# Four unread matmuls on the tensor engine ahead of the first product behind each of six norms

## The chip, the cores and the metric

The kernel runs as one program on one core of a Trainium2 chip. The metric is the device time of one execution in microseconds (us), as the median of several runs. The engines of the core are named as the profile names them: PE is the tensor engine's matmuls and PEld its weight loads, DVE the vector engine, ACT the scalar engine, POOL the GpSimd engine, SP the engine whose queue carries the weight transfers. PE works at one of two granted clock levels, 2.4 GHz (written as 1.00 in the profile) and 1.2 GHz (0.50).

## What the reference computes

The input x has 512 tokens of 1024 features in float32. It goes through six blocks one after the other, each as a residual:

```python
h = h + nsa_mixer(rmsnorm(h, l0_norm))          # attention, three branches
h = h + s5_mixer(rmsnorm(h, l1_norm))           # state-space scan
h = rmsnorm(h, final_norm)
h = h + even_mixer(rms_norm(h, mix_norm_g[0]))  # stick-breaking and retention
h = h + conv_ffn(rms_norm(h, ffn_norm_g[0]))
h = h + odd_mixer(rms_norm(h, mix_norm_g[1]))   # gated linear attention
h = h + conv_ffn(rms_norm(h, ffn_norm_g[1]))
```

A norm is `x * rsqrt(mean(x*x) + 1e-6) * gain` over the features of a token. Seven norms stand in the program; six of them are followed at once by a large product with a weight matrix (`w_in` of the four mixers, `w_up` of the two feed-forward layers), and one, the final norm of the first half, is followed by another norm.

## The kernel before, in words

**Layout.** All activations are kept feature-major: `h` is 128 partitions by 8 chunks by 512 tokens. Sums over features are matmuls with a 128x128 matrix of ones (`ones`, a part of the tile `tables`), which leave the sum on every partition.

**Products.** The weights come as tiles of 128 outputs (128 x 1024 numbers, 512 KB). SP loads them into a ring of four buffers `raw` (line 131). DVE rounds a tile to `whi` (line 155) and POOL forms the rest `wlo = raw - whi` (line 149); both are double buffered. The activations are split in the same way into `xh` and `xl`. One output tile is then 8 chunks of three matmuls, `whi*xh`, `whi*xl`, `wlo*xh`, 24 in all, into one of two accumulators `acc[0]`, `acc[1]`, which are banks 0 and 1. A tile's end is counted on `tile_done`, on which DVE waits to round the tile after next, and ACT or DVE to take the accumulator; whoever takes it counts on `acc_free`.

**Norms.** ACT squares the chunks of `h` (line 202), DVE adds them up in `ssq` (line 215). At a stage's end `pe_squares` (lines 217 to 224) multiplies `ones` by `ssq` and by the last square, two matmuls in plain float32. In the profile one plain float32 matmul shows as two records. `act_rstd` takes the logarithm and the exponential (lines 232, 234). Then `dve_norm` (line 251 makes `xf`, line 255 makes `xl`) and `act_norm_split` (line 241 makes `xh`) go through the 8 chunks in four rounds of two, with two buffers `xf`.

**The first products.** `products_from_norm` (line 258) issues the first four tiles of the stage behind a norm. In its first tile every chunk waits for that chunk's `xl` (the semaphore `norm_lo`); lines 269, 270 and 271 are its three matmuls. It is called for six stages: `nsa_kv`, `s5_in`, `even_in`, `up0`, `odd_in`, `up1`. What PE has in its program just ahead of the call differs:

- `nsa_kv`: 32 plain float32 matmuls for the gates (line 1033), each chunk's behind its `xf`; they all stand ahead of the call.
- `even_in`: a wait for three transfers of tables, `pe.wait_ge(e_loaded, 48)` (line 554). ACT issues them behind its share of the norm (lines 651 to 653).
- `odd_in`: the gate matmul (line 1563) of each chunk is inside the call, ahead of that chunk's three matmuls of the first tile. DVE waits for it (semaphore `o_gmm`) before it writes that `xf` buffer again.
- `s5_in`, `up0`, `up1`: nothing but `pe_squares`.

PE's program is one stream in order, so whatever stands in it is done before what follows it.

Of the kernel before, what the change touches and what calls it, by code (L numbers as in the profile page):

```python
# [36 lines left out]
def plan(names):  # L37

    t0, o0, n, t, o = {}, {}, {}, 0, 0
    for name, tiles, per_output in STAGES:  # L40
        if name not in names:
            continue
        t0[name], o0[name], n[name] = t, o, tiles
        t, o = t + tiles, o + tiles // per_output
    return t0, o0, n, t


def build(nc, A, out, names=tuple(s[0] for s in STAGES)):
    T0, O0, NT, TILES = plan(names)
# [4 lines left out]
    with ExitStack() as ctx:  # L54
        def sb(name, shape, dt=F32):
            return ctx.enter_context(nc.sbuf_tensor(name, shape, dt))

        def sem(name):
            return ctx.enter_context(nc.semaphore(name))
# [3 lines left out]
        acc = bank[0:2]  # L63
        ssum = bank[7]

        h = sb("h", [P, KC, S])
# [13 lines left out]
        ones = tables[:, 0:P]  # L80
# [18 lines left out]
        acc_free = [sem("acc_free0"), sem("acc_free1")]  # L99
# [143 lines left out]
        def dve_norm(dve, n, view=lambda x: x, reader=None):  # L243

            dve.wait_ge(rstd_ready, n + 1)
            with dve.Fori(0, KC // 2) as i:
# [6 lines left out]
                for j in range(2):  # L253
                    dve.wait_ge(norm_hi, i * 2 + (8 * SPLIT[n] + j + 1))
                    nc.vector.tensor_tensor(chunk(xl, i * 2 + j), xf[:, j, :], chunk(xh, i * 2 + j).bitcast(F32),
                                            ALU.subtract).then_inc(norm_lo, 1)

        def products_from_norm(pe, stage, n, beside=None, between=None):

            for j in range(4):  # L260
                pe.wait_ge(w_lo, T0[stage] + j + 1)
                pe.wait_ge(acc_free[j % 2], (O0[stage] + j) // 2 + 1)
                for k in range(KC):
                    if j == 0:
                        if beside is not None:
                            beside(k)
                        pe.wait_ge(norm_lo, 8 * SPLIT[n] + k + 3)
                    w_h, w_l = whi[:, j % 2, k * P:(k + 1) * P], wlo[:, j % 2, k * P:(k + 1) * P]
                    nc.tensor.matmul(acc[j % 2][:], w_h, xh[:, k, :], start=k == 0, stop=False)  # L269
                    nc.tensor.matmul(acc[j % 2][:], w_h, xl[:, k, :], start=False, stop=False)  # L270
                    mm = nc.tensor.matmul(acc[j % 2][:], w_l, xh[:, k, :], start=False, stop=k == KC - 1)  # L271
                mm.then_inc(tile_done, 1)
                if between is not None:
                    between(j)
# [65 lines left out]
        def pe_ffn(pe, layer):  # L340
            products_from_norm(pe, f"up{layer}", ORDER[(N_FFN0, N_FFN1)[layer]])
            products_feature_major(pe, f"up{layer}", 4, 2 * FT - 4)
            third = FT - 2 * KC
            rhs = [(lambda k, q=q: ghi[:, q * KC + k, :], lambda k, q=q: glo[:, q * KC + k, :]) for q in range(3)]
            after = ORDER[(N_FFN0, N_FFN1)[layer]] + 1
            pe_residual(pe, f"down{layer}", after if after < len(norms) else None,
                        lambda k: pe.wait_ge(g_lo, FT * layer + k + 1), 3, rhs, (KC, KC, third))
# [205 lines left out]
        def pe_even(pe):  # L553
            pe.wait_ge(e_loaded, 48)
            products_from_norm(pe, "even_in", ORDER[N_MIX0], between=lambda j: pe_head_squares(pe, 0) if j == 2 else None)
            parts = iter(range(16, 28 * 4))

            def beside(n):
                for _ in range(n):
                    product_beside(pe, "even_in", 0, 0, 4, next(parts))  # L560

            for i in range(4):
                pe_stick(pe, i, beside)
                pe_retention(pe, i, beside if i < 3 else lambda n: pe_even_out_beside(pe, n))
# [461 lines left out]
        def pe_nsa(pe):  # L1026
# [11 lines left out]
            for m in range(KC):  # L1038
                gate(m)
            products_from_norm(pe, "nsa_kv", n)  # L1040
            products_feature_major(pe, "nsa_kv", 4, 4)

# [1648 lines left out]
```

## Time and profile before

| | |
|---|---|
| median of 3 runs | 2185.01 us (2181.14 to 2190.68) |
| the profiled execution's own time | 2186.51 us |
| its span, first to last instruction | 2184.7 us |
| mean granted PE clock | 0.964 |
| PE busy | 92% of the span |
| DVE, ACT, POOL busy | 53%, 32%, 37% |

The span is 1.8 us shorter than the execution's own time, and that execution is 1.5 us above the median. Times in a timeline are counted from the span's start. A row of a timeline gives start, duration, engine, line, operation and tiles, and in brackets how long the engine sat idle before it and what ended that. The duration of a matmul record holds the time its last column takes to come out; the distance of two starts is what a matmul costs in a row of them.

### The profile page before, as it was taken

To read this page: it belongs to the slowest core of one execution; us is meant where nothing else is said; L and a number is where in the kernel's file an instruction comes from. 1 tells how busy PE (TensorE), PEld (TensorE's weight loads), DVE (VectorE), ACT (ScalarE), POOL (GpSimd) and SP (SyncE) were. 2 spreads that over 40 slices of the span, in tenths; PEclk is the share of its full clock that TensorE was granted. 3 is DMA by queue.
4 is the path that set the end of the run, shared out by engine and by line. 5 is a ranking of instruction groups with operands and counts; after the bars stand their busy time and mean duration, and the time that the engine had idled before them with its cause. 6 is when DMAs were issued, how large, how long until landed. Compare 5 with 4: busy or idle time off the path is not lost.

```text
span 2184.7 us, 28177 instructions
## 1 busy us (share of the span) xinstructions
PE 2004.5 (92%) x9960; PEld 1574.4 (72%) x9960; DVE 1155.3 (53%) x2011; ACT 697.6 (32%) x1284; POOL 799.1 (37%) x412
## 2 busy tenths in 40 slices
PE   5999999777999985999988999999998898999999
PEld 4777777656777764666666888888586676888887
DVE  5728998676994443555535555522513435555411
ACT  2125655223552122444413333300313423333200
POOL 1451221234773431222223444444242133444443
PEclk8999999898999997999989999999999999999999
DMA  3630110211211221111112222233221022222232
GB/s 116 171 109 30 40 40 20 77 61 54 68 33 68 96 87 63 58 58 59 58 49 79 96 96 96 96 106 106 69 87 58 29 70 77 96 96 96 96 125 77
DMA packets 55150, 167.56 MB, mean 77 GB/s; under 512 B 8065, under 2 KB 16129, under 8 KB 54801
## 3 DMA queue, kind: packets, MB, share of 16 engines
q1 hardware_dynamic: 47760, 155.22, 21.2%
q10 hardware_dynamic: 7296, 11.08, 1.8%
q8 instruction: 62, 1.02, 0.2%
q14 instruction: 32, 0.25, 0.0%
HBM read 157.88 MB, written 2.10 MB: 73 GB/s over the span
## 4 chain that ended last, share of the span: by engine, by line
PE 56%; issue 24%; DVE 11%; POOL 6%; ACT 1%; ACTq 1%; DMA 0%; DVEq 0%; POOLq 0%
PE bank L164 13%; PE bank L166 13%; PE bank L165 13%; POOL wlo L149 6%; DVE prob L1416 2%; DVE ssb L1403 2%; PE bank L269 1%; PE bank L270 1%; PE bank L271 1%; DVE sb__137 L2078 1%; PE bank L1135 1%; DVE sb__137 L2073 1%; PE bank L492 1%; PE bank L1160 1%; PE bank L493 1%
## 5 line engine op out<-in xcount | busy, mean ns | idle before, releaser
L149 POOL TENSOR_TENSOR wlo<-raw,whi 128x1024 fp32r<-128x1024 f32 x260 | 626.6, 2410 | 1134.4 <-DVE whi L155 1134.4
L155 DVE CAST whi<-raw 128x1024 fp32r<-128x1024 f32 x288 | 202.7, 704 | 641.4 <-PE bank L166 449.4
L164 PE MATMUL bank<-xh,whi 128*128 128x512 f32 x832 | 328.1, 394 | 12.9 <-POOL wlo L149 9.7
L165 PE MATMUL bank<-xl,whi 128*128 128x512 f32 x832 | 326.5, 392 | 0.0
L166 PE MATMUL bank<-xh,wlo 128*128 128x512 f32 x832 | 326.2, 392 | 0.0
L164 PEld LDWEIGHTS bank<-xh,whi 128*128 128x128 f32 x832 | 157.9, 190 | 48.3 <-POOL wlo L149 11.4
L166 PEld LDWEIGHTS bank<-xh,wlo 128*128 128x128 f32 x832 | 157.9, 190 | 33.4
L165 PEld LDWEIGHTS bank<-xl,whi 128*128 128x128 f32 x832 | 158.1, 190 | 32.7
L492 PE MATMUL bank<-xh,whi 128*128 128x512 f32 x328 | 140.5, 428 | 2.2 <-ACT oin L478 1.2
L164 PE MATMUL bank<-ghi,whi 128*128 128x512 f32 x352 | 136.9, 389 | 0.0
L166 PE MATMUL bank<-ghi,wlo 128*128 128x512 f32 x352 | 136.9, 389 | 0.0
L165 PE MATMUL bank<-glo,whi 128*128 128x512 f32 x352 | 136.9, 389 | 0.0
L494 PE MATMUL bank<-xh,wlo 128*128 128x512 f32 x328 | 129.4, 394 | 0.0
L493 PE MATMUL bank<-xl,whi 128*128 128x512 f32 x328 | 129.2, 394 | 0.0
L269 PE MATMUL bank<-xh,whi 128*128 128x512 f32 x192 | 83.2, 433 | 38.2 <-DMA swap<-in_swap_dram 19.5
L381 DVE SCALAR_TENSOR_TENSOR c<-upad,cw,c 128x512 f32<-128x512 f32 x44 | 77.0, 1750 | 56.0 <-ACT c L361 56.0
L1464 POOL TENSOR_TENSOR wlo<-raw,whi 128x1024 fp32r<-128x1024 f32 x20 | 47.2, 2361 | 149.2 <-DVE whi L155 149.2
L202 ACT ACTIVATE bank<-h 128x512 f32<-128x512 f32 x42 | 25.2, 601 | 220.2 <-DVE h L306 212.5
L1416 DVE TENSOR_SCALAR prob<-prob,gsig,stat 128x128 f32<-128x128 f32 (+3 forms) x128 | 87.2, 723 | 2.3
L391 DVE TENSOR_TENSOR glo<-gf,ghi 128x512 f32 x44 | 66.1, 1501 | 40.9 <-ACT ghi L366 40.9
L269 PEld LDWEIGHTS bank<-xh,whi 128*128 128x128 f32 x192 | 38.7, 201 | 64.8 <-DMA swap<-in_swap_dram 21.1
L492 PEld LDWEIGHTS bank<-xh,whi 128*128 128x128 f32 x328 | 62.4, 190 | 24.9 <-issue 11.6
(362 smaller groups left out, 3962.5 us busy)
## 6 DMA issues: line engine op xcount, KB each, us to landing
raw<-in_weights_dram SPq DMA_DIRECT2D x288, 512.0 KB, 3.6
h<-in_x_dram SPq DMA_DIRECT2D x1, 2048.0 KB, 8.3
sz<-su SPq DMA_DIRECT2D x128, 16.0 KB, 1.8
out_dram<-h ACTq DMA_DIRECT2D x4, 512.0 KB, 3.2
etab<-in_even_tables_dram ACTq DMA_DIRECT2D x1, 1730.0 KB, 6.4
x_kh<-kvc_h ACTq DMA_DIRECT2D x2, 256.0 KB, 4.0
x_kl<-kvc_l ACTq DMA_DIRECT2D x2, 256.0 KB, 5.5
x_vh<-kvc_h ACTq DMA_DIRECT2D x2, 256.0 KB, 8.3
```

The source lines that it names most:

```text
L149: nc.gpsimd.tensor_tensor(wlo[:, s % 2, :], raw[:, s, :], whi[:, s % 2, :].bitcast(F32), ALU.subtract).then_inc(w_lo, 1)
L155: nc.vector.tensor_copy(whi[:, t_of_4 % 2, :], raw[:, t_of_4, :]).then_inc(w_hi, 1)
L164: nc.tensor.matmul(to, w_h, pe_h, start=first and k == 0, stop=False)
L165: nc.tensor.matmul(to, w_h, pe_l, start=False, stop=False)
L166: last_mm = nc.tensor.matmul(to, w_l, pe_h, start=False, stop=last and k == chunks - 1)
L269: nc.tensor.matmul(acc[j % 2][:], w_h, xh[:, k, :], start=k == 0, stop=False)
L381: nc.vector.scalar_tensor_tensor(c1[:], upad[:, 1:1 + S], cw[:, layer, 1, ds(i * 2 + j, 1)], c0[:], ALU.mult, ALU.add).then_inc(conv1, 1)
L391: nc.vector.tensor_tensor(chunk(glo, i * 2 + j), gf[:], chunk(ghi, i * 2 + j).bitcast(F32), ALU.subtract).then_inc(g_lo, 1)
L492: nc.tensor.matmul(to[:], w_h, xh[:, k, :], start=k == 0, stop=False)
L493: nc.tensor.matmul(to[:], w_h, xl[:, k, :], start=False, stop=False)
L494: mm = nc.tensor.matmul(to[:], w_l, xh[:, k, :], start=False, stop=k == KC - 1)
L1416: mul = nc.vector.tensor_scalar(prob[:, br, hd, 0:w], prob[:, br, hd, 0:w], gsig[:, qb, g:g + 1], stat[:, 8 + 2 * br + hd:9 + 2 * br + hd] ...
```

## The change

A function `pe_keep_busy` is called first in `products_from_norm`, so at all six stages. It waits until the accumulator `acc[0]` is free, which the first product would wait for too, and issues four plain float32 matmuls of `ones` by the first chunk of `h` into it, each of 128x128 by 128x512 and each beginning a new sum. Nobody reads them; the first product begins with `start=True` and overwrites them. Nothing else changes.

```diff
+        KEEP = 4
+
+        def pe_keep_busy(pe, stage):
+
+            pe.wait_ge(acc_free[0], O0[stage] // 2 + 1)
+            for _ in range(KEEP):
+                nc.tensor.matmul(acc[0][:], ones, h[:, 0, :], start=True, stop=True)
+
         def products_from_norm(pe, stage, n, beside=None, between=None):
 
+            pe_keep_busy(pe, stage)
             for j in range(4):
                 pe.wait_ge(w_lo, T0[stage] + j + 1)
                 pe.wait_ge(acc_free[j % 2], (O0[stage] + j) // 2 + 1)
```

## Rows read from the trace of the kernel before

**Rows 1.** The page: busy shares, and the granted clock in 40 slices.

```profile
PE 2004.5 (92%) x9960; PEld 1574.4 (72%) x9960; DVE 1155.3 (53%) x2011; ACT 697.6 (32%) x1284; POOL 799.1 (37%) x412
...
PEclk8999999898999997999989999999999999999999
```

**Rows 2.** The waits of PE: us in total, times, longest.

```profile
PE bank L222 <- DVE ssq L215: 44.7, 7, 23.7
PE bank L269 <- DMA swap<-in_swap_dram: 19.5, 1, 19.5
```

**Rows 3.** Timeline behind the last norm, stage `up1`.

```profile
1811.57 1.02 PE L224 MATMUL bank<-sq,tables 128*128 128x512 f32 x2
...
1816.84 0.76 PE L269 MATMUL bank<-xh,whi 128*128 128x512 f32 x1 [4.25 <-DVE xl L255]
...
1822.60 0.52 PE L269 MATMUL bank<-xh,whi 128*128 128x512 f32 x1
...
1824.77 1.37 DVE L255 TENSOR_TENSOR xl<-xf,xh 128x512 f32 x2 [0.23 <-ACT xh L241]
...
1825.52 0.50 PE L269 MATMUL bank<-xh,whi 128*128 128x512 f32 x1 [1.26 <-DVE xl L255]
```

**Rows 4.** Timeline: plain float32 matmuls of 512 columns.

```profile
823.94 1.91 PE L224 MATMUL bank<-sq,tables 128*128 128x512 f32 x2
...
1555.45 3.69 PE L1572 MATMUL bank<-gas,walpha 16*128 16x512 f32 x8
```

**Rows 5.** Timeline: the first products of `nsa_kv` and `even_in`.

```profile
44.49 0.77 PE L269 MATMUL bank<-xh,whi 128*128 128x512 f32 x1
...
845.38 0.80 PE L269 MATMUL bank<-xh,whi 128*128 128x512 f32 x1 [19.53 <-DMA swap<-in_swap_dram]
...
851.01 0.40 PE L269 MATMUL bank<-xh,whi 128*128 128x512 f32 x1
851.24 0.39 PE L270 MATMUL bank<-xl,whi 128*128 128x512 f32 x1
```

**Rows 6.** Timeline behind the norm of `s5_in`.

```profile
457.12 1.67 PE L224 MATMUL bank<-sq,tables 128*128 128x512 f32 x2
...
463.05 0.77 PE L269 MATMUL bank<-xh,whi 128*128 128x512 f32 x1 [4.27 <-DVE xl L255]
```

**Rows 7.** Timeline behind the norm of `odd_in`.

```profile
1534.66 1.02 PE L224 MATMUL bank<-sq,tables 128*128 128x512 f32 x2
...
1539.06 1.59 PE L1563 MATMUL bank<-xf,wga 128*16 128x512 f32 x2 [3.38 <-DVE xf L251]
...
1542.15 1.33 PE L1563 MATMUL bank<-xf,wga 128*16 128x512 f32 x2
...
1543.67 0.75 DVE L251 SCALAR_TENSOR_TENSOR xf<-h,gains,rstd 128x512 f32<-128x512 f32 x1 [1.80 <-PE bank L1563]
```

**Rows 8.** Stretches between two times: busy us by engine, granted clock.

```profile
core 0: us, PE busy (x) PEld busy (x) DVE busy (x) ACT busy (x) POOL busy (x), PEclk, DMA share, GB/s
...
44.40:47.70 3.30, 3.30 (x10) 2.62 (x10) 2.71 (x13) 0.52 (x4) 0.00 (x0) 0.50 0.00 0
...
463.00:467.50 4.50, 4.22 (x9) 2.96 (x10) 4.01 (x7) 1.31 (x3) 0.00 (x0) 0.50 0.01 2
...
822.50:825.90 3.40, 3.35 (x4) 0.74 (x3) 0.00 (x0) 0.83 (x2) 0.00 (x0) 0.50 0.00 0
825.90:829.30 3.40, 0.00 (x0) 0.00 (x0) 1.46 (x3) 2.07 (x4) 0.00 (x0) 0.99 0.00 0
...
845.30:849.80 4.50, 4.42 (x10) 3.51 (x11) 0.00 (x0) 0.00 (x0) 0.00 (x0) 0.50 0.00 0
...
1167.60:1170.60 3.00, 2.91 (x7) 1.90 (x7) 2.77 (x5) 1.26 (x2) 0.00 (x0) 0.50 0.00 0
...
1815.80:1822.60 6.80, 5.76 (x13) 3.64 (x13) 6.14 (x10) 3.21 (x6) 0.00 (x0) 0.50 0.00 0
1822.60:1828.00 5.40, 4.13 (x17) 3.01 (x18) 3.62 (x7) 1.96 (x3) 0.00 (x0) 0.99 0.06 17
```

## The prediction, made before the changed kernel was run

> **What bounds the kernel now.** I read the page first: PE is busy for 92% of the span and its granted clock is below 9 tenths in only a few slices [rows 1]. So the tensor engine sets the time nearly everywhere, and each us put into its stream where it doesn't wait is a us of the kernel. Next I read whom PE waits for. The pauses ahead of the sum of squares are not touched, since the new matmuls come behind it; the one long wait the change stands near is 19.5 us for the transfer of `swap` ahead of `even_in` [rows 2]. Then I read the timeline behind each of the six norms and asked two questions: is PE idle at the place where the new matmuls stand in its program, and is it PE that sets the pace behind them.
>
> Behind the last norm (`up1`) the second record of the sum of squares starts 0.43 us behind the first, at 1812.0, and makes room for the next at 1812.4. The first product starts at 1816.84. That is the pause the change means, 4.4 us. What follows is not paced by PE: the chunks of the first tile come in pairs, at 1822.60 and again at 1825.52, one pair in 2.92 us, because DVE and ACT make them so; PE waits 1.26 us for the last pair [rows 3]. A pair is six matmuls. They take 6 x 0.23 = 1.4 us at the full clock (two starts 0.23 us apart, [rows 5]), and 6 x 0.44 = 2.6 us at the half clock (10 in 4.42 us, [rows 8]). Both are less than 2.92. So the half clock that the trace shows there, from 1815.8 to 1822.6 [rows 8], delays nothing: the first tile ends when DVE's last `xl`, of the row at 1824.77, is there [rows 3].
>
> **The change, part by part.** It removes nothing. It adds four plain float32 matmuls at six places, a read of `h` that nobody writes there, and a wait for `acc[0]` that the first product has as well and that is fulfilled long before, so I cost it at nothing.
>
> The price of four such matmuls: eight records of exactly this kind, 512 columns one behind the other, took 3.69 us, of which some 0.2 us is the last one coming out, at the full clock; so 8 x 0.43 = 3.4 us [rows 4]. That row has 16 partitions in place of 128; the pair of records of the sum of squares, 1.02 us for two at the full clock [rows 3], gives the same 0.43. At the half clock two records took 1.91 us [rows 4], so a record is 0.85 and the four matmuls 6.8 us.
>
> Now by place.
>
> `nsa_kv`. The 32 gate matmuls stand ahead of the call, and PE goes from them into the first product at 44.49 with no idle time [rows 5]. There is no pause left: every record of the new matmuls lies on the path. The clock is at half until 47.7 [rows 8]. If it rises at the same time as before, the work added is 8 records in an unchanged stretch of slow clock: 3.2 us at half take 3.8 records, the other 4.2 take 1.8 us at full, and the products that had run at half now run at full. Net, the delay is the price at full clock, **+3.4 us**. Bounds: 0 if something behind it has that much slack, 6.8 if the clock rises only later. I take 3.4, as PE's stream behind it is dense and DVE's side work there hangs on each tile's end.
>
> `even_in`. The wait for the tables stands ahead of the call, so the pause of 19.5 us isn't filled at all: the new matmuls start where the first product did, at 845.4, on a cold engine [rows 2, 5]. The clock was at half until 849.8 and then full [rows 8]. By the same working: **+3.4 us**, bounds 0 and 6.8.
>
> `s5_in`. The sum of squares ran partly at half clock, and the next record can start at about 458.6 (the row at 457.12 lasts 1.67 us, less the 0.2 that the last takes to come out). The first product waits for `xl` until 463.05, so there are 4.4 us [rows 6]. At full clock the four fit; at half they would end at 465.4, 2.4 us late. A dense pass of such records did lift the clock before: it was at 0.50 over the sum of squares from 822.5 to 825.9 and at 0.99 right behind it, with no other matmul near [rows 8]. So I expect a rise within the pass, near 460.7, and an end at 463.1. And were it late, the first tile catches up: a pair costs PE 1.4 to 2.6 us and comes every 3. **+0.1 us**, bounds 0 and 0.5.
>
> `up0` and `up1`. 3.4 us in a pause of 4.4 at the full clock: they end a us before the first product. The clock behind them is full in place of half, in a part that DVE and ACT pace. **0 us** each. The cover is the pace of the norm, 2.92 us a pair; without it, the half clock over 13 records from 1815.8 [rows 8] would be worth 13 x 0.21 = 2.7 us, and over 7 records at `up0` 1.5 us.
>
> `odd_in`. The sum of squares makes room at 1535.5, and the first gate starts at 1539.06 [rows 7]. 1535.5 + 3.4 = 1538.9: they just fit. Here the clock matters: each gate is a plain float32 matmul, and DVE waits for the second (start 1542.15, 1.33 us) before it can write `xf` again at 1543.67, having been idle for 1.80 us [rows 7]. That gate ran late because the gate and the product ahead of it ran at half clock. At the full clock the first product, which starts at 1540.58 once its `xl` is there, takes 0.8 us, then the gate 1.0: the `xf` starts at about 1542.7. **-1.0 us**, bounds -1.5 and +0.5.
>
> The sum: 3.4 + 3.4 + 0.1 + 0 - 1.0 + 0 = **+5.9 us**. Against the profiled execution's own 2186.5 that is 2192.4; that execution was 1.5 us above the median, so the median becomes 2185.0 + 5.9 = **2190.9 us**, +0.27%. A measurement of this kernel can tell about 0.5%, 10.9 us, from no change, and three runs of the same kernel lay 9.5 us apart; so this is within what counts as no change.
>
> The Trainium skill bears on this: its page TensorE: Matmul & The Clock Gate, section Why this matters for your kernels, advises to leave no long idle gap between bursts of matmuls so that the clock doesn't fall. The trace agrees that the clock falls behind the norms, and shows besides that the slow stretch is covered there by the norm's own pace; by the page alone each slow stretch would be time to win.
>
> **The rivals.**
>
> A. The clock pays behind every norm, since the pace of the norm isn't as firm as I read it. Then the slow stretches are won back: 2.7 us at `up1`, 1.5 at `up0`, 9 records from 463.0 at `s5_in` [rows 8] 1.9, and 1.0 at `odd_in`: -7.1, against +6.8 for the two places on the path: -0.3, 2184.7 us. For it: the slow pair, 2.6 us and the 0.1 to 0.2 of its first record, is close under 2.92. Against it: PE's wait of 1.26 us for the last pair [rows 3]. This is the way that the page's rule gives. Chance 0.10.
>
> B. **Slower.** The new matmuls lift or hold the clock too early. The slow stretch then comes later, no longer in the paced first tile but in the dense tiles behind it, because the paced tile has gaps. A slow stretch as at `up1`, 6.8 us, over dense products holds 16 matmuls, each 0.21 us dearer: 3.4 us a place. At `s5_in`, `up0`, `odd_in` and `up1`: 5.9 + 4 x 3.4 = +19.5, 2204.5 us. It decides from the second place on (5.9 + 6.8 = 12.7, over 10.9). Against it: the clock stayed at 0.99 over the gappy stretch from 1822.6, PE busy 4.13 of 5.40 us [rows 8]. For it: the stretch would now start two pairs earlier, and nothing shows what the clock does then. Chance 0.10.
>
> C. The new matmuls don't lift a slow clock, and the two on the path cost 6.8 each with the products' slow stretch still behind them: +13.6 and nothing won at `odd_in`, 2198.6 us. Against it is the rise behind 822.5 to 825.9 [rows 8]. Chance 0.05.
>
> D. The delays at `nsa_kv` and `even_in` are taken up by slack further on: about -1, 2184 us. Against it: 92% busy [rows 1], and all later work hangs on those tiles. Chance 0.05.
>
> E. Something shortens the run by more than 0.5%. The slow clock near the norms holds nowhere near 10.9 us that could be won; only a lucky shift of other slow stretches could. Chance 0.04.
>
> **How the numbers follow.** The forecast keeps 0.66. Its own spread is that of the runs, 2181 to 2191, half of which I allow around 2190.9; so a twelfth of it may be measured over +10.9. Slower by over 0.5%: B 0.10, C 0.05, 0.05 of the forecast: 0.20. Faster: 0.04. The same: 0.76. The range reaches down to rivals A and D, 2184, and up to C, 2199; B and E are left out with some of the spread.
>
> **What would show it.** In the changed kernel's profile: 48 new records in all, 8 at each place; those of `nsa_kv` right behind the gates and those of `even_in` right behind the wait for `swap`, with the first product some 5 us behind their start and the stage's end 3.4 us later than before; at `up0` and `up1` the first product still about 4.4 us behind the sum of squares, the pairs still 2.92 us apart and the clock full; at `odd_in` DVE's second wait for the gate shortened from 1.80 us to under 1. I am wrong if the first tile at `up0` or `up1` ends nearer to the sum of squares than before (A), if a slow stretch shows in tiles 1 to 3 of those stages (B), or if the records of `nsa_kv` are 0.85 us apart to the last (C).

## The result, and the profile after

The changed kernel took **2197.9 us** in the median (2191.5 to 2206.4, 12 runs), the kernel before 2186.5 us beside it (12 runs). The ratio is 1.0051, with a 95% interval of 1.0039 to 1.0064: +11.2 us, from +8.5 to +14.0. The forecast was 2190.9, +5.9. The time lies in the range given, and the sign of the sum was right; but the measured size is nearly double the one forecast, and it sits right at the 0.5% below which the forecast counted a difference as no change. One term of the sum, that of `odd_in`, had the wrong sign.

The page of the changed kernel, its span, busy shares and granted clock:

```profile
span 2196.8 us, 28273 instructions
...
PE 2021.6 (92%) x10008; PEld 1577.8 (72%) x10008; DVE 1154.7 (53%) x2011; ACT 698.0 (32%) x1284; POOL 800.5 (36%) x412
...
PEclk8999999998999997999989999999999999999999
```

PE has 48 records more than in [rows 1], is busy 17 us longer, and the span is 12.1 us longer. By stage, from one sum of squares to the next, these are +2.8 us at `nsa_kv`, -2.4 at `s5_in`, +6.8 at `even_in`, 0.0 at `up0`, +4.1 at `odd_in` and +0.9 behind that of `up1`; the -2.4 is no gain of the change, since stages that a kernel does not touch differ by as much from profile to profile (see the end). The mean granted clock rose, from 0.964 to 0.968. A higher clock and a busier engine go together here with a slower kernel: the engine is busy with work that nobody reads.

What the new records (line 264; the lines behind it have moved by 9) waited for, in the answer on that line:

```profile
L264 PE MATMUL bank<-h,tables x48: 592/592/1222, 44.3 to 1828.4; 128*128 128x512 f32 x48
its engine sat idle before it (us, times) until:
  DMA swap<-in_swap_dram: 41.2, 2
...
  DMA obias<-in_odd_bias_dram: 7.4, 2
```

The reader should see two transfers here, not one (each is counted for PE and for PEld). The wait for `swap` was forecast. The wait for `obias`, the last of the tables of `odd_in`, was not: it stands in the program just as the one of `even_in` does.

The timeline, the new records and what follows them, place by place:

```profile
44.28 5.47 PE L264 MATMUL bank<-h,tables 128*128 128x512 f32 x8
...
49.19 0.79 PE L278 MATMUL bank<-xh,whi 128*128 128x512 f32 x1
...
460.69 3.60 PE L264 MATMUL bank<-h,tables 128*128 128x512 f32 x8
...
465.12 0.47 PE L278 MATMUL bank<-xh,whi 128*128 128x512 f32 x1 [0.84 <-DVE xl L255]
...
846.02 5.69 PE L264 MATMUL bank<-h,tables 128*128 128x512 f32 x8 [19.82 <-DMA swap<-in_swap_dram]
...
851.15 0.80 PE L278 MATMUL bank<-xh,whi 128*128 128x512 f32 x1
...
1170.39 3.60 PE L264 MATMUL bank<-h,tables 128*128 128x512 f32 x8
...
1174.81 0.47 PE L278 MATMUL bank<-xh,whi 128*128 128x512 f32 x1 [0.82 <-DVE xl L255]
...
1546.08 5.40 PE L264 MATMUL bank<-h,tables 128*128 128x512 f32 x8 [3.27 <-DMA obias<-in_odd_bias_dram]
...
1551.41 1.03 PE L1572 MATMUL bank<-xf,wga 128*16 128x512 f32 x2
...
1552.63 0.75 DVE L251 SCALAR_TENSOR_TENSOR xf<-h,gains,rstd 128x512 f32<-128x512 f32 x1 [4.42 <-PE bank L1572]
...
1824.46 4.50 PE L264 MATMUL bank<-h,tables 128*128 128x512 f32 x8
...
1828.92 0.47 PE L278 MATMUL bank<-xh,whi 128*128 128x512 f32 x1
```

At 460.69 and 1170.39 the eight records take 3.60 us and PE still waits 0.8 us for the norm: the pause held them. At 44.28, 846.02 and 1546.08 the next matmul of the program comes straight behind them, with no idle time. At 1824.46 (`up1`) too, but there the records began 2.6 us behind the start of the sum of squares in place of 1.8 and took 4.50 us at a clock that was partly low; `e2_odd` below, which adds nothing at `up1`, had its first product there even later. At 1546.08 the records also ran at the half clock in part, after PE had stood for 3.27 us. DVE now waits for the first gate, 4.42 us, where it did not wait at all before, and then 1.10 us for the second, where [rows 7] had 1.80.

Stretches of the changed kernel, columns as in [rows 8]:

```profile
44.20:47.60 3.40, 3.40 (x6) 1.56 (x6) 2.68 (x13) 0.52 (x4) 0.00 (x0) 0.50 0.02 5
47.60:52.00 4.40, 4.40 (x16) 2.79 (x15) 0.00 (x0) 0.00 (x0) 0.00 (x0) 0.96 0.00 0
846.00:849.70 3.70, 3.67 (x5) 1.61 (x6) 0.00 (x0) 0.00 (x0) 0.00 (x0) 0.50 0.00 0
...
1170.40:1174.80 4.40, 3.59 (x9) 1.35 (x8) 2.25 (x4) 2.58 (x4) 0.00 (x0) 1.00 0.40 119
1174.80:1185.20 10.40, 6.70 (x25) 4.39 (x26) 8.63 (x14) 3.78 (x6) 0.00 (x0) 1.00 0.04 10
1185.20:1205.00 19.80, 19.80 (x89) 16.36 (x88) 11.63 (x12) 7.63 (x10) 9.60 (x4) 1.00 0.24 79
...
1544.00:1551.20 7.20, 5.12 (x8) 2.01 (x8) 2.78 (x4) 1.95 (x4) 0.00 (x0) 0.76 0.18 68
```

The slow stretch behind the norm of `up0` is gone, as the change meant: 1.00 from 1174.8 on, where [rows 8] had 0.50 for 3 us. The tile ended no sooner for it, as this table shows (the e-rows are the experiments of the next section). It gives how long behind the sum of squares (the start of line 222's matmul) the second tile of the stage began, from the timelines of one profile each:

| us | nsa_kv | s5_in | even_in | up0 | odd_in | up1 |
|---|---|---|---|---|---|---|
| before | 27.9 | 17.6 | 31.0 | 16.4 | 25.3 | 16.4 |
| changed | 31.4 | 16.9 | 34.5 | 16.4 | 29.0 | 17.2 |
| e1_pauses | 28.6 | 16.9 | 30.8 | 16.9 | 26.7 | 18.0 |
| e2_odd | 28.9 | 18.1 | 31.0 | 16.9 | 26.9 | 18.1 |
| e3_nsa_even | 32.6 | 17.6 | 34.1 | 17.0 | 26.5 | 18.0 |
| e10_nsa | 31.7 | 16.9 | 30.6 | 15.9 | 25.4 | 17.2 |
| e11_even | 29.0 | 18.3 | 34.4 | 16.9 | 26.5 | 17.4 |
| e4_ahead | 27.4 | 17.5 | 31.1 | 16.4 | 24.3 | 17.2 |
| e7_keep16 | 28.7 | 21.0 | 30.8 | 22.7 | 25.2 | 22.7 |

Places where a kernel adds nothing scatter by up to 1.7 us, because the clock in the sum of squares, the gates or the first tile differs from profile to profile; +3.5, +3.5 and +3.7 us at the three places with something ahead of the call stand out of that. At `odd_in` the kernel before is near the low end of the profiles that add nothing there (25.2 to 26.7), so the +3.7 is 2.3 to 3.8 us against them.

### The profile page after: what moved, and what is told of

Read it like the earlier page. It is cut to its first block, busy times and chain, and to the rows that moved or that the text cites. A ratio compares the mean times of both kernels' runs of the same rounds, so it can differ in the third digit from the quotient of the medians.

```text
span 2196.8 us, 28273 instructions
## 1 busy us (share of the span) xinstructions
PE 2021.6 (92%) x10008; PEld 1577.8 (72%) x10008; DVE 1154.7 (53%) x2011; ACT 698.0 (32%) x1284; POOL 800.5 (36%) x412
## 4 chain that ended last, share of the span: by engine, by line
PE 54%; issue 23%; DVE 12%; POOL 6%; SPq 2%; ACT 1%; DMA 1%; ACTq 1%; DVEq 0%; POOLq 0%
PE bank L164 13%; PE bank L166 12%; PE bank L165 12%; POOL wlo L149 6%; SPq L141 2%; DVE prob L1425 2%; DVE ssb L1412 2%; PE bank L278 1%; PE bank L280 1%; PE bank L279 1%; DVE sb__137 L2087 1%; DVE sb__137 L2082 1%; PE bank L1144 1%; PE bank L1169 1%; PE bank L501 1%
## 5 line engine op out<-in xcount | busy, mean ns | idle before, releaser
L164 PEld LDWEIGHTS bank<-xh,whi 128*128 128x128 f32 x832 | 157.7, 189 | 47.8 <-POOL wlo L149 10.7
L165 PEld LDWEIGHTS bank<-xl,whi 128*128 128x128 f32 x832 | 157.9, 190 | 32.6
L202 ACT ACTIVATE bank<-h 128x512 f32<-128x512 f32 x42 | 25.2, 601 | 219.0 <-DVE h L315 211.3
L501 PEld LDWEIGHTS bank<-xh,whi 128*128 128x128 f32 x328 | 62.6, 191 | 25.0 <-issue 11.6
L165 PEld LDWEIGHTS bank<-glo,whi 128*128 128x128 f32 x352 | 66.1, 188 | 13.8
```

The costliest lines, as they stand in the source:

```text
L164: nc.tensor.matmul(to, w_h, pe_h, start=first and k == 0, stop=False)
L165: nc.tensor.matmul(to, w_h, pe_l, start=False, stop=False)
L501: nc.tensor.matmul(to[:], w_h, xh[:, k, :], start=k == 0, stop=False)
```

## The experiments

Two theories were set against each other. **The place**: the four matmuls cost their time where PE's own program has a wait or other matmuls just ahead of the call, so that they begin when the first product (or gate) could have begun; they cost nothing where only the sum of squares is ahead and the norm paces the first tile. **The clock**: the slow stretch behind a norm costs PE time that a busy engine wins back, or (the other sign) the new matmuls move slow stretches to dense products. Ratios below are against the kernel before on the same chip, with the 95% interval, and turned into us with 2186.

### Only the three true pauses

```diff
-            pe_keep_busy(pe, stage)
+            if stage in ("s5_in", "up0", "up1"):
+                pe_keep_busy(pe, stage)
```

> The four matmuls stand only at s5_in, up0 and up1, where nothing but the sum of squares is ahead of them. Theory of the place (the matmuls cost where PE's program has a wait or other matmuls just ahead of the call, and nothing where the norm paces the first tile): 0 us within the measurement, -2 to +2; first products at up0 and up1 6.2 us behind the start of the sum of squares as before, the clock full behind them. Theory of the clock (the slow stretch behind a norm costs PE time and is won back): about -6 us. Theory of the displaced slow stretch (rival B): +7 to +10 us.

Measured (e1_pauses): ratio 1.0002 (0.9992 to 1.0011), +0.4 us (-1.7 to +2.4). The clock's -6 and rival B's +7 to +10 are both outside. The pauses hold the matmuls, and the full clock behind them is worth nothing there that these runs could tell from zero. One detail was expected wrongly: the first products at `up0` and `up1` came 6.7 and 7.9 us behind the start of the sum of squares, not 6.2. They did so in `e2_odd` as well (6.8 and 7.9), which adds nothing there; the sum of squares ran partly at the half clock in both.

### Only `odd_in`, and only `nsa_kv` and `even_in`

The same edit, with `("odd_in",)` and with `("nsa_kv", "even_in")`.

> The four matmuls stand only at odd_in, behind the wait for its tables. Theory of the place: the first gate is late by the matmuls' time less what is left of the pause, the stage from one sum of squares to the next grows by about 4 us, and the kernel by +3.5 to +5. As predicted blind (the matmuls start right behind the sum of squares): -1 us. Theory of the clock: -1 to -2 us.

Measured (e2_odd): 1.0010 (1.0001 to 1.0019), +2.2 us (+0.2 to +4.2), less than the +3.5 to +5 expected, and not the gain that was predicted. Its timeline at that place:

```profile
1535.46 3.70 PE L264 MATMUL bank<-h,tables 128*128 128x512 f32 x8 [1.56 <-DMA obias<-in_odd_bias_dram]
...
1539.09 1.03 PE L1573 MATMUL bank<-xf,wga 128*16 128x512 f32 x2
```

Here PE had stood for 1.56 us only, since the sum of squares ahead of it ran slow and ended later; the eight records took 3.70 us where the changed kernel's took 5.40. So this place costs more or less with the clock that it meets: the second tile began 1.6 us later than in [rows 7]'s kernel here, 3.7 us in the changed kernel. Against the other profiles that add nothing at `odd_in` the 1.6 us do not stand out (26.9 against up to 26.7), and the whole stage, expected some 4 us longer, was 0.1 us longer in this profile; that the place costs something rests on the times of the runs and on the changed kernel's profile.

> The four matmuls stand only at nsa_kv and even_in. Theory of the place: 3.4 us each, +6.8 us in all (+5.5 to +8). If even_in costs more than its 8 records, as its stage in the changed kernel's profile (6.8 us longer) could mean: +9 to +11. If slack further on takes the delay up: 0 to +3.

Measured (e3_nsa_even): 1.0032 (1.0018 to 1.0046), +7.0 us (+3.9 to +10.1), as the place theory has it. The two alone:

> The four matmuls at nsa_kv alone, behind the gates. Theory of the place: +3.4 us (the second tile begins 3.4 us later behind the sum of squares, and nothing further on takes it up), +2.5 to +4.5. If nsa_kv and even_in don't share the measured +7 us equally, it shows here: 0 or +7.

Measured (e10_nsa): 1.0008 (0.9997 to 1.0019), +1.7 us (-0.7 to +4.2). The interval holds both 0 and the 3.4. In its profile the second tile began 3.8 us later, but the stage to the next sum of squares was only 0.5 us longer than in the kernel before, and such a stage scatters by about 3 us. So this run does not exclude that part of the delay is taken up further on.

> The four matmuls at even_in alone, behind the wait for the tables. Theory of the place: +3.4 us, +2.5 to +4.5. If the 6.8 us by which the stage was longer in the changed kernel's profile belong to these matmuls: +6 to +7.

Measured (e11_even): 1.0012 (1.0003 to 1.0020), +2.6 us (+0.7 to +4.4). The 6.8 us by which the stage was longer in the changed kernel's profile are thus not all of these matmuls. In that profile the clock fell twice within the stage at places where it hadn't before; this row catches one, more than 100 us behind the nearest new record, and the row below it the same place in e1_pauses, which adds nothing at `even_in` or `nsa_kv`:

```profile
961.00:964.50 3.50, 3.14 (x6) 1.61 (x7) 2.80 (x7) 1.81 (x4) 1.25 (x1) 0.74 0.00 0
...
955.50:961.50 6.00, 5.85 (x15) 3.23 (x16) 3.46 (x8) 2.02 (x5) 2.35 (x1) 0.72 0.08 11
```

The same falls stand in the profiles of e3_nsa_even and e11_even, and in that of e7_keep16, which adds nothing at `even_in` either. They are not a mark of the new records.

### All six, moved ahead of the waits and the gates

```diff
         def pe_nsa(pe):
...
+            pe_keep_busy(pe, "nsa_kv")
             pe.wait_ge(n_loaded, 64)
             for m in range(KC):
                 gate(m)
...
         def pe_even(pe):
+            pe_keep_busy(pe, "even_in")
             pe.wait_ge(e_loaded, 48)
...
         def pe_odd(pe):
...
+            pe_keep_busy(pe, "odd_in")
             pe.wait_ge(o_loaded, 64)
```

The three others stay in `products_from_norm`, as in the first experiment. This is the same number of matmuls as in the changed kernel.

> The four matmuls stand at all six stages, but at nsa_kv, even_in and odd_in they are moved ahead of the waits for tables and ahead of the gates, right behind the sum of squares. Theory of the place: all six are covered; 0 us at five and up to -1 us at odd_in, whose gates then run at the full clock: -2 to +2 us in all. If the cost of the changed kernel is one of matmuls as such, by the slow stretches that they move or by their reads, it stays: +8 to +12 us.

Measured (e4_ahead): 0.9996 (0.9985 to 1.0008), -0.9 us (-3.3 to +1.7). This decides between the theories: the same 48 records stand in the program, and the +11.2 us is gone. What cost was the place. Timeline at `odd_in`, to be read against [rows 7]:

```profile
1535.05 3.60 PE L264 MATMUL bank<-h,tables 128*128 128x512 f32 x8
...
1538.58 1.03 PE L1575 MATMUL bank<-xf,wga 128*16 128x512 f32 x2
...
1542.20 0.75 DVE L251 SCALAR_TENSOR_TENSOR xf<-h,gains,rstd 128x512 f32<-128x512 f32 x1 [0.80 <-PE bank L1575]
```

The matmuls begin right behind the sum of squares, the first gate comes 5.3 us behind the start of that sum as in the kernel before, and DVE waits 0.80 us in place of 1.80. The second tile begins 1.0 us sooner than before. That is what the prediction had worked out for this place; it had the matmuls on the wrong side of a wait. The 1.0 us is one profile's; over the runs it is inside the interval.

### Sixteen in place of four in the three pauses

```diff
-        KEEP = 4
+        KEEP = 16
```

together with the edit of the first experiment.

> Sixteen matmuls in place of four, at s5_in, up0 and up1 only: 32 records, 13.7 us at the full clock, against 4.4 us of pause. Theory of the place with the norm's pace as cover: the first product is late by 9 to 10 us, then the first tile runs dense (24 x 0.23 = 5.5 us in place of some 11 us at the norm's pace), so the tile ends 3.5 to 4 us late: +10 to +12 us over three places. If the norm's pace gives no cover: +28 us, what stands beyond the pauses. If matmuls are costed by their time alone: +41 us.

Measured (e7_keep16): 1.0087 (1.0073 to 1.0101), +19.0 us (+16.0 to +22.1). It is less than the +28 without cover and far from +41, but more than the +10 to +12 expected. Timeline at `up1`:

```profile
1822.29 14.71 PE L264 MATMUL bank<-h,tables 128*128 128x512 f32 x32
...
1836.44 0.80 PE L279 MATMUL bank<-xh,whi 128*128 128x512 f32 x1
```

The records began 2.7 us behind the start of the sum of squares, not 1.8, and took 14.7 us, not 13.9, as the clock was low at their start; the tile then ran dense, 5.9 us, and the next began 6.3 us later than before, as at `up0`, and 3.4 us later at `s5_in`. These are 16.0 of the 19.0 us. The cover is there: first products that were 8.2 to 10.6 us late became second tiles 3.4 to 6.3 us late. What the expectation missed at two of the places is the clock: 0.9 us of later start, 0.8 of longer filler and 0.4 in the tile.

### Filling the long pause of `even_in`

The kernel before, with this alone:

```diff
+            for _ in range(20):
+                nc.tensor.matmul(acc[0][:], ones, h[:, 0, :], start=True, stop=True)
             pe.wait_ge(e_loaded, 48)
```

> The kernel before with twenty unread matmuls at even_in alone, ahead of the wait for the tables, so that they fill nearly the whole pause (40 records, 17 us at the full clock, from 825.6 to about 843). The ten products that ran at half clock from 845.4 then run at full: 10 x 0.21 = -2 us, if a filled pause pays where dense products follow. If the clock doesn't matter: 0. If it falls all the same in the last 2.5 us: 0.

Measured (e8_even_fill): 0.9990 (0.9981 to 1.0000), -2.2 us (-4.2 to 0.0). The size fits the -2 expected, but the profile of this kernel shows the third case of the expectation and not the gain: the first product, 2.91 us behind the end of the filler, met a clock that fell again under it.

```profile
828.00:845.00 17.00, 17.00 (x41) 7.42 (x39) 10.86 (x16) 6.36 (x10) 0.00 (x0) 1.00 0.22 72
845.00:847.50 2.50, 0.36 (x1) 0.00 (x0) 0.00 (x0) 0.00 (x0) 0.00 (x0) 1.00 0.63 245
847.50:850.00 2.50, 1.74 (x4) 1.45 (x5) 0.00 (x0) 0.00 (x0) 0.00 (x0) 0.66 0.02 4
```

Whether a filled pause pays at the one place where dense products follow is left open at this size: one profile says no, the interval touches zero.

### Taking the pause away in place of filling it

PE waits at `even_in` for tables that the first three tiles don't read. In e5_even_wait the kernel before has the wait moved:

```diff
         def pe_even(pe):
-            pe.wait_ge(e_loaded, 48)
-            products_from_norm(pe, "even_in", ORDER[N_MIX0], between=lambda j: pe_head_squares(pe, 0) if j == 2 else None)
+            def between(j):
+                if j == 2:
+                    pe.wait_ge(e_loaded, 48)
+                    pe_head_squares(pe, 0)
+
+            products_from_norm(pe, "even_in", ORDER[N_MIX0], between=between)
```

> The kernel before with one wait moved: PE's wait for the tables of the even mixer stands behind the third tile of even_in, ahead of the first matmul that reads a table, in place of ahead of the first tile. No added matmuls. If PE's wait for the tables is the long pause of that stage, as read: the first product starts when the norm gives its first chunk, near 830.0 in place of 845.4, and the first two tiles are done when ACT has its tables and takes them; the third tile starts some 11 to 12 us earlier: -11 to -12 us. If ACT's own wait for the same tables sets the stage: 0 to -3 us.

Measured (e5_even_wait): 0.9950 (0.9937 to 0.9964), -10.9 us (-13.8 to -7.9), just under what was expected. The timeline of PE and ACT has the steps as expected:

```profile
829.34 0.76 PE L269 MATMUL bank<-xh,whi 128*128 128x512 f32 x1 [4.24 <-DVE xl L255]
...
844.99 0.60 ACT L635 ACTIVATE et<-bank 128x512 f32<-128x512 f32 x1 [7.18 <-DMA swap<-in_swap_dram]
```

The first product came 8.0 us behind the sum of squares in place of 23.3, PE did two tiles, ACT took both once the tables had landed, and the third tile began 11.5 us earlier than before. In e6_even_early ACT also issues the three loads earlier:

```diff
+                if name == "even":
+                    act.dma_start(etab[:], A["even_tables"]).then_inc(e_loaded, 16)
+                    act.dma_start(egain[:], A["even_gains"]).then_inc(e_loaded, 16)
+                    act.dma_start(swap[:], A["swap"]).then_inc(e_loaded, 16)
                 act_rstd(act, n)
...
         def act_even(act):
-            act.dma_start(etab[:], A["even_tables"]).then_inc(e_loaded, 16)
-            act.dma_start(egain[:], A["even_gains"]).then_inc(e_loaded, 16)
-            act.dma_start(swap[:], A["swap"]).then_inc(e_loaded, 16)
```

> As e5_even_wait, and ACT issues the three loads of the tables ahead of the norm's logarithm in place of behind its share of the norm, so they land before the first tile ends. ACT then takes the first tile at once: -12 to -13.5 us against the kernel before, about 1 us better than e5_even_wait. If the loads are late for another reason (transfers of weights ahead of them): no better than e5_even_wait.

Measured (e6_even_early): 0.9936 (0.9923 to 0.9950), -14.0 us (-16.8 to -10.9), 3 us better than e5_even_wait where about 1 was expected. Timeline of ACT and its queue:

```profile
820.98 0.45 ACTq L2449 DMA_DIRECT2D swap<-in_swap_dram  x1
...
839.24 0.60 ACT L635 ACTIVATE et<-bank 128x512 f32<-128x512 f32 x1 [1.96 <-PE bank L271]
```

The loads go out 17 us earlier than in the kernel before, ACT no longer waits for them, and takes the first tile when PE ends it; the third tile begins 13.5 us earlier than before. The same kernel once more, on another chip:

> The kernel of e6_even_early once more, on the same chip as e9_best, to compare the two: -14 us again.

Measured (e6b_again): 0.9947 (0.9934 to 0.9960), -11.6 us (-14.4 to -8.7), not the -14 expected again: its median is 2175.9 us here and was 2171.9 on the other chip, while the kernel before took 2187.0 and 2186.8. And with four unread matmuls at `odd_in` alone, ahead of the wait for `o_loaded`:

> e6_even_early (the even tables loaded ahead of the norm, PE's wait for them behind the third tile) and four unread matmuls at odd_in alone, ahead of the wait for its tables. Theory of the place: covered there, and the gates run at the full clock, which ended the first tile 1.0 us sooner in the profile of e4_ahead: -1 us against e6_even_early, so -15 us against the kernel before. If the clock at the gates is worth nothing over many runs: the same as e6_even_early, -14 us.

Measured (e9_best): 0.9936 (0.9923 to 0.9948), -14.0 us; beside e6b_again on the same chip its median is 2.2 us lower (2173.7 against 2175.9, five runs each). Each of its five runs is shorter than each of the other's five, so that difference is clear of the scatter of runs. But it is one pair on one chip, and the same kernel differed by 4.0 us between two chips; that the 2.2 us are the work of the four matmuls at `odd_in` is likely from the profile of e4_ahead and not shown. The version without them has nearly all of the gain.

## Why the prediction was right or wrong

**`odd_in`: wrong, and the step that failed.** The prediction let the four matmuls start right behind the sum of squares, at 1535.5, so that they just fit before the first gate at 1539.06. PE's program has `pe.wait_ge(o_loaded, 64)` between the two, and the prediction and the list of what stands ahead of the call both miss it. The row of PE in [rows 7] puts the idle time of 3.38 us down to DVE's `xf`, which came last. The wait for the tables is still in the trace of before, just above that row, at the weight load of the same matmul:

```profile
1539.03 0.12 PEld L1563 LDWEIGHTS bank<-xf,wga 128*16 128x16 f32 x2 [4.18 <-DMA obias<-in_odd_bias_dram]
```

So the tables were there 5.3 us behind the start of the sum of squares (5.2 in the changed kernel, 4.8 in e2_odd), a moment ahead of the gate, and nothing was left of the pause for work that stands behind the wait. Forecast -1.0; the profile of the changed kernel shows +3.7 there, the kernel with this place alone +2.2. With the measured value in place of -1.0 the sum is 3.4 + 3.4 + 0.1 + 2.2 = +9.1, in the interval.

The other half of that term, the gain at the gates, was sound. The first gate came 3.1 us later than before in e2_odd and 5.2 in the changed kernel, but from the first gate to the second tile it took 18.5 us in both in place of 20.0, as the gates met a full clock. So the place costs the matmuls' time less some 1.5 us given back, which is why e2_odd came out under its expected +3.5 to +5.

**`nsa_kv` and `even_in`: right for the two together.** +3.4 each was forecast; the second tile began 3.5 us later at both, and both together gave +7.0. Alone they gave +1.7 (-0.7 to +4.2) and +2.6 (+0.7 to +4.4): each interval holds the 3.4, and the first holds zero. The argument held that a stretch of slow clock which stays where it was makes the added work cost its price at the full clock. The records at 44.28 took 5.47 us, yet the delay was 3.5, since the products behind them no longer ran slow.

**`s5_in`, `up0`, `up1`: right.** +0.1 forecast, +0.4 (-1.7 to +2.4) measured for the three together. The cover was the norm's pace, and the sixteen matmuls showed how far it reaches.

**The rivals.** A, the way that the Trainium skill's advice gives, fell: with the slow stretches gone at the three pauses (1.00 from 1174.8), nothing was won. The Trainium skill's page TensorE: Matmul & The Clock Gate, section Why this matters for your kernels, advises against long idle gaps between bursts; its effect on the clock is seen here, its effect on the time is not, because the tile behind each gap is paced by DVE and ACT. B fell with the same rows and with the +0.4 us of the three places: the clock held at 1.00 over the gappy first tile, PE busy 6.70 of 10.40 us, and over the dense tiles behind it, to 1205.0. C fell: the clock rose within the new matmuls' stretch at 47.6, right where it had. D, slack further on, has the +7.0 against it as a whole; a part of it, at `nsa_kv` above all, is not excluded by the +1.7 measured there.

**What stays open.** All six measured +11.2 (8.5 to 14.0); the parts give 0.4 + 2.2 + 7.0 = 9.6, or 6.9 with `nsa_kv` and `even_in` taken singly. The intervals overlap, and a difference of some 2 to 4 us may be real. `odd_in` was dearer in the changed kernel's profile than alone: there PE had stood for 3.27 us ahead of the new records and they took 5.40 us, in e2_odd it had stood for 1.56 and they took 3.70. Two profiles do not show that the one is the cause of the other, and no run tells which case most executions are.

## What to carry to other kernels

Filler matmuls begin where they stand in the engine's program, not where the profile shows a pause: list every wait and every matmul between the last useful instruction and the place, also those that the matmul's own row does not name because another wait ended a moment later. Its weight load's row can name them, as it did here. A slow clock is worth fighting only where the engine itself sets the pace, as at the gates of `odd_in` (18.5 us in place of 20.0); behind a norm that hands out one pair of chunks in 2.92 us, six matmuls fit at either clock. And a pause is better removed than filled: moving one wait and three loads gave 11 to 14 us where filling the same pause gave about 2, if anything.

## What the runs showed of the hardware that was not expected

How the slow stretches fall differs from execution to execution of one kernel. The sum of squares ran at the full clock in one profile and partly at the half clock in another of the same stage (its second half took 1.02 us in [rows 3] and 1.86 us in the changed kernel, at 1822.81), the four matmuls at `up0` and `up1` took 3.6 to 4.8 us over the profiles, and the first product of `even_in` met a falling clock though PE had been busy for 17 us until 2.9 us before it. A stage that a kernel doesn't touch was up to some 3 us longer or shorter than in the kernel before. So a single profile can't price anything under 3 us here. Eight to twelve runs still left intervals of 2 to 3 us to either side, and the distance from one engine's own landmark to the next, as in the table, scattered by up to 1.7.
